# Two-layer hybrid mixer block on one core: halved filler units, two interleaved output units, bias rows read from PSUM, and four early units in the last norm

## The chip, the cores and the metric

The kernel runs on one core of a Trainium2 chip. The metric is the device time of one execution in microseconds, as the median of several runs. Lower is better.

## What is computed

Two layers of a transformer-like block over 256 latent tokens `x` and 256 context tokens `h`, model width 1024, hidden width 2816. Each layer has a half-step SwiGLU FFN, a token mixer and a second half-step SwiGLU FFN, each behind an RMS norm that is modulated per channel by vectors computed from `c` and `c_ctx`:

```python
x = x + 0.5 * mx[2] * swiglu(modulate(rms_norm(x, norm_ffn1[l]), mx[0], mx[1]), ffn1_w_in[l], ffn1_w_out[l])
ux = modulate(rms_norm(x, norm_mix[l]), mx[3], mx[4])
yx, yh = token_mixer(ux, uh, w_in[l], ...)
x = x + mx[5] * yx
x = x + 0.5 * mx[8] * swiglu(modulate(rms_norm(x, norm_ffn2[l]), mx[6], mx[7]), ffn2_w_in[l], ffn2_w_out[l])
```

The mixer projects its input once (`w_in`), runs three branches (a Fourier mix, grouped-query attention with 8 heads, neighbourhood attention with 4 heads), maps each to width 1024, merges them with three sigmoid gates computed from the same input, and multiplies by `w_o`. The context tokens go the same way in layer 0. In layer 1 they only supply keys and values, so most work there has 256 columns and not 512. A final RMS norm of `x` is the output.

## The kernel before

**Layout.** Activations are held with channels on partitions: `x`, `u_hi`, `u_lo` are 128 x 8 x 512 (latent tokens in columns 0 to 255, context in 256 to 511). Each weight block is one "unit" of 128 output channels: up to eight 128x128 blocks, 512 KB. Every product is made of three matmuls for the precision (`three_of`, L1286 to L1288): `w_hi*u_hi`, `w_hi*u_lo`, `w_lo*u_hi`. A unit of eight blocks is 24 matmuls.

**The weight ring.** Units pass in one fixed order through a ring of four slots. SyncE loads `w_raw`; ScalarE copies it to `w_hi` (`hi`, L526), which waits for the load and for TensorE to be done with the unit four places earlier (`w_used`); GpSimd subtracts to get `w_lo` (L494, two instructions of 128x512 for a unit, `w_lo_ready`); TensorE uses both. ScalarE's and VectorE's programs are written out in order, with the `hi` calls between the other work.

**Norms.** A norm is made without waiting for its root: while the layer's last product arrives in `x`, ScalarE and VectorE write `x * colA` as a pair (`first_scaled` L548, `first_split` L906), and TensorE runs the first two units of the next product (`pair` with `early`) on it, with two extra columns for the shift. `mean_square` (L1366), a root on ScalarE, and `spread` (L1373) give 1/rms on all partitions; then VectorE and ScalarE make the normalised operand `u_hi`, `u_lo` in eight steps (`norm`, L930, L581, L943). For an FFN the two early results are scaled at their eviction (`first_hidden`, L1017, L1023), and the product goes to `h_hi`, `h_lo` (L1005, L1007). TensorE's third step onward waits for `h_prod`; a shortcut for that step to wait only for the scaled halves applies where the step's number is a constant of the program. In the last norm (`k` = 5, the second FFN of layer 1, 256 tokens) the early pair lies in `u_hi`, `u_lo` itself.

**Attention.** The jobs go two at a time. Step `p` has, on TensorE: the transposes of the last step's first job, this step's scores, the transposes of the last step's second job, then units named by `between(l)` as fillers ("before"), the value matmuls of the last step (L1653), and more fillers ("after"). VectorE copies the transposed probabilities (L1199), takes maxima (L1155, L1156), and normalises (L1188); every second step in layer 0 and every step in layer 1 it also evicts a finished chunk to `cat_hi`, `cat_lo` (L1140, L1141). ScalarE copies the other half, takes the exponentials (L767), and evicts the fillers from bank 7 after them. In layer 0 even steps have the latent stream (512 keys) and odd ones the context stream (256 keys); steps 8 to 11 are the neighbourhood jobs, whose latent stream adds a bias first. The fillers are the remaining projections (`nk`, `nq`, `nv`, two each), the transposition of v (`vt`) and the first three gate units:

```python
return [([nk0], [nk1]), ([], []), ([nq0], []), ([], []), ([nq1], []), ([], []),
        ([nv0], [("vt", 1)]), ([nv1], [("vt", 2)]), ([g0], []), ([], []), ([g1], []), ([], []), ([g2], [])]
```

**Merge.** Eight gate steps follow; each ends with VectorE's merge (L1233, L1236, L1238, L1241, L1243) into one chunk of `mg_hi`, `mg_lo`. `w_o`'s first unit takes the chunks in order and so waits for the last; seven more units follow, alternating between banks 2 and 3, and each is added to `x` (`update`, L983), squared (L541), summed (L898) and split for the next norm (L906). ScalarE converts one unit of `w_o` in each of these steps.

**Start.** The per-channel rows (`vec`) are transposed into PSUM and copied to SBUF; `columns_norm(0)` (L876 to L878) combines them with the first modulation columns, and the first norm follows.

## Time and profile before

| | |
|---|---|
| median of 3 runs | 2025.54 us (2023.0 to 2025.99) |
| profiled execution, device time | 2022.01 us |
| its span, first to last instruction | 2020.2 us |
| mean granted TensorE clock | 0.996 |
| TensorE busy | 1962.2 us (97%) |
| weight loads busy | 1609.4 us (80%) |
| GpSimd busy | 1006.0 us (50%) |
| VectorE busy | 773.1 us (38%) |
| ScalarE busy | 655.2 us (32%) |

The profile is of one execution. Times inside it are microseconds from its first instruction. The busy time of an engine counts instructions in progress. Matmuls overlap each other, so their mean duration is longer than the step from one to the next. A granted clock of 1.00 is 2.4 GHz on TensorE and 0.50 is 1.2 GHz.

### The profile page before, as it was taken

To read this page: it belongs to the slowest core of one execution; us is meant where nothing else is said; L and a number is where in the kernel's file an instruction comes from. 1 tells how busy PE (TensorE), PEld (TensorE's weight loads), DVE (VectorE), ACT (ScalarE), POOL (GpSimd) and SP (SyncE) were. 2 spreads that over 40 slices of the span, in tenths; PEclk is the share of its full clock that TensorE was granted. 3 is DMA by queue.
4 is the path that set the end of the run, shared out by engine and by line. 5 is a ranking of instruction groups with operands and counts; after the bars stand their busy time and mean duration, and the time that the engine had idled before them with its cause. 6 is when DMAs were issued, how large, how long until landed. Compare 5 with 4: busy or idle time off the path is not lost.

```text
span 2020.2 us, 29286 instructions
## 1 busy us (share of the span) xinstructions
PE 1962.2 (97%) x10550; PEld 1609.4 (80%) x10550; DVE 773.1 (38%) x1278; ACT 655.2 (32%) x1031; POOL 1006.0 (50%) x835
## 2 busy tenths in 40 slices
PE   6999999999999999999999999999999899999998
PEld 4777777787667888877877887788778677998998
DVE  4322122357762224623122353221233875564214
ACT  3211211243452223412211243222123444444433
POOL 2444444343213544545544445454445433988997
PEclk9999999999999999999999999999999999999999
DMA  9555655343112333553354236434523422655664
GB/s 338 171 179 181 195 189 181 122 113 108 43 43 64 102 94 94 172 183 114 117 165 129 72 112 224 159 96 142 179 67 105 142 75 58 183 166 158 184 181 131
DMA packets 413575, 279.25 MB, mean 138 GB/s; under 512 B 25346, under 2 KB 398588, under 8 KB 406060
## 3 DMA queue, kind: packets, MB, share of 16 engines
q1 hardware_dynamic: 401868, 206.79, 34.6%
q10 hardware_dynamic: 11520, 71.05, 9.6%
q8 instruction: 62, 1.02, 0.2%
q14 instruction: 29, 0.24, 0.0%
q0 software_dynamic: 96, 0.16, 0.0%
HBM read 276.92 MB, written 1.05 MB: 138 GB/s over the span
## 4 chain that ended last, share of the span: by engine, by line
PE 84%; POOL 5%; issue 5%; DVE 4%; DMA 1%; ACT 1%; SPq 0%; POOLq 0%; DVEq 0%; ACTq 0%
PE bank L1286 26%; PE bank L1287 26%; PE bank L1288 25%; POOL w_lo L494 5%; PE bank L1395 3%; DVE u_lo L943 1%; PE bank L1653 1%; PE bank L1635 1%; PE bank L1588 1%; DMA w_raw<-in_ffn_w_in 1%; DVE tmp L930 1%; DVE rstd L1112 1%; PE bank L1535 1%; DVE qk L1103 0%; SPq L403 0%
## 5 line engine op out<-in xcount | busy, mean ns | idle before, releaser
L494 POOL TENSOR_TENSOR w_lo<-w_raw,w_hi 128x512 fp32r<-128x512 f32 (+2 forms) x824 | 1003.4, 1247 | 1003.0 <-ACT w_hi L526 1002.2
L1286 PE MATMUL bank<-u_hi,w_hi 128*128 128x512 f32 (+2 forms) x2008 | 723.2, 360 | 16.6 <-DVE u_lo L943 12.4
L1287 PE MATMUL bank<-u_lo,w_hi 128*128 128x512 f32 (+2 forms) x2008 | 713.7, 355 | 0.0
L1288 PE MATMUL bank<-u_hi,w_lo 128*128 128x512 f32 (+2 forms) x2008 | 712.9, 355 | 0.0
L1286 PEld LDWEIGHTS bank<-u_hi,w_hi 128*128 128x128 f32 x2008 | 380.6, 190 | 97.1 <-DVE hf L999 21.0
L526 ACT ACTIVATE w_hi<-w_raw 128x1024 fp32r<-128x1024 f32 (+2 forms) x412 | 385.3, 968 | 178.1 <-PE bank L1288 164.3
L1288 PEld LDWEIGHTS bank<-u_hi,w_lo 128*128 128x128 f32 x2008 | 380.5, 189 | 53.9
L1287 PEld LDWEIGHTS bank<-u_lo,w_hi 128*128 128x128 f32 x2008 | 380.9, 190 | 52.3 <-issue 0.8
L999 DVE TENSOR_TENSOR hf<-bank,sg 128x512 f32<-128x512 f32 (+1 forms) x85 | 53.2, 625 | 613.5 <-ACT sg L628 613.5
L1286 PE MATMUL bank<-h_hi,w_hi 128*128 128x512 f32 (+1 forms) x704 | 256.0, 364 | 0.0
L1287 PE MATMUL bank<-h_lo,w_hi 128*128 128x512 f32 (+1 forms) x704 | 255.4, 363 | 0.0
L1288 PE MATMUL bank<-h_hi,w_lo 128*128 128x512 f32 (+1 forms) x704 | 255.2, 363 | 0.0
L628 ACT ACTIVATE sg<-bank 128x512 f32<-128x512 f32 (+1 forms) x85 | 46.3, 544 | 638.3 <-PE bank L1288 638.3
L983 DVE SCALAR_TENSOR_TENSOR x<-bank,colG,x 128x256 f32<-128x256 f32 (+1 forms) x136 | 60.6, 480 | 276.3 <-PE bank L1288 275.7
L1286 PEld LDWEIGHTS bank<-h_hi,w_hi 128*128 128x128 f32 x704 | 132.9, 189 | 25.6 <-DVE x L983 5.0
L1288 PEld LDWEIGHTS bank<-h_hi,w_lo 128*128 128x128 f32 x704 | 132.9, 189 | 20.7
L1287 PEld LDWEIGHTS bank<-h_lo,w_hi 128*128 128x128 f32 x704 | 132.9, 189 | 20.4
L1007 DVE TENSOR_TENSOR h_lo<-hf,h_hi 128x512 fp32r<-128x512 f32 (+2 forms) x88 | 125.5, 1426 | 4.6
L541 ACT ACTIVATE sq<-x 128x512 f32<-128x512 f32 (+3 forms) x48 | 26.9, 560 | 179.4 <-DVE x L983 179.3
L1233 DVE TENSOR_TENSOR tmp<-bank,sig 128x512 f32<-128x512 f32 (+1 forms) x42 | 20.8, 551 | 161.5 <-PE bank L1288 161.5
L814 ACT ACTIVATE sig<-bank 128x512 f32<-128x512 f32 (+1 forms) x42 | 20.6, 491 | 160.0 <-PE bank L1288 160.0
L1395 PE MATMUL bank<-mod_w,sil 128*32 128x512 f32 x512 | 61.6, 598 | 0.0
(170 smaller groups left out, 1523.7 us busy)
## 6 DMA issues: line engine op xcount, KB each, us to landing
w_raw<-in_ffn_w_in SPq DMA_DIRECT2D x176, 512.0 KB, 3.8
mod_w<-in_mod_w ACTq DMA_DIRECT2D x56, 1024.0 KB, 6.9
w_raw<-in_w_in SPq DMA_DIRECT2D x68, 512.0 KB, 3.7
w_raw<-in_ffn_w_out SPq DMA_DIRECT2D x64, 384.0 KB, 3.4
w_raw<-in_ffn_w_out SPq DMA_DIRECT2D x64, 320.0 KB, 3.3
mod_first<-in_mod_w SPq DMA_DIRECT2D x4, 2048.0 KB, 14.3
mod_w<-in_mod_w ACTq DMA_DIRECT2D x16, 512.0 KB, 5.5
w_raw<-in_w_o SPq DMA_DIRECT2D x16, 512.0 KB, 4.2
```

What stands on the lines that cost most here:

```text
L494: pool.tensor_tensor(w_lo[:, slot, k0:k1, :], w_raw[:, slot, k0:k1, :], w_hi[:, slot, k0:k1, :].bitcast(F32), ALU.subtract).then_inc(S("w_ ...
L526: act.activation(w_hi[:, slot, 0:n, :], w_raw[:, slot, 0:n, :], ACT.Copy).then_inc(S("w_hi_ready"), 1)
L541: act.activation(sq[:, par, 0:n], x[:, bass.ds(m, 1), 0:n].rearrange("p a n -> p (a n)"), ACT.Square).then_inc(S("sq_ready"), 1)
L628: act.activation(sg[:, b, 0:n], bank[:, 2 * b + 1, 0:n], ACT.Silu).then_inc(S("silu_ready"), 1)
L983: last = dve.scalar_tensor_tensor(out=xs, in0=bank[:, b, cols], scalar=colG[:, k, v, bass.ds(m, 1)], in1=xs, op0=ALU.mult, op1=ALU.add)
L999: dve.tensor_tensor(hf[:, b, 0:n], bank[:, 2 * b, 0:n], sg[:, b, 0:n], ALU.mult).then_inc(S("h_prod"), 1)
L1007: dve.tensor_tensor(h_lo[:, bass.ds(s, 1), 0:n].rearrange("p a n -> p (a n)"), hf[:, b, 0:n], hs.bitcast(F32), ALU.subtract).then_inc(S("h ...
L1233: last = dve.tensor_tensor(tmp[:, j, 0:n], bank[:, 3 + j, 0:n], gates, ALU.mult)
L1286: pe.matmul(dst, w_hi[:, slot, kk, :], hi_, start=start, stop=False)
L1287: pe.matmul(dst, w_hi[:, slot, kk, :], lo_, start=False, stop=False)
L1288: return pe.matmul(dst, w_lo[:, slot, kk, :], hi_, start=False, stop=stop)
L1395: last = pe.matmul(bank[32 * q:32 * q + 32, 6, :].rearrange("p (a i) -> p a i", i=32), sil[:, 2 * b + par, :], w[:, q], start=b == 0 and p ...
```

## The change

- `between(l)` names three lists per step ("middle" comes between the two transpose groups), and most fillers are cut in two halves of four weight blocks (12 matmuls) each, which go to neighbouring steps. Bank 7 holds the sum between them, and the unit is evicted after its second half.
- `w_o`'s first two units run interleaved, block by block, on banks 2 and 6. ScalarE converts `w_o`'s third and fourth unit ahead of the first update of `x`, and stays one unit further ahead; the following phase's third unit is converted in the last step.
- `columns_norm(0)` reads the rows from PSUM (bank 4) and no longer from the copy in SBUF.
- In the last norm four units (two FFN steps) run on `x * colA`. It lies in its own tiles (`first_hi_m`, `first_lo_m`), and both steps are scaled at eviction, both scalings ahead of the first product.

```diff
         if l == DEPTH - 1:
-            return [([nk0], [nk1]), ([nq0], [nq1]), ([nv0], [("vt", 1)]), ([nv1], [("vt", 2)]), ([g0], []), ([g1], []), ([g2], [])]
-        return [([nk0], [nk1]), ([], []), ([nq0], []), ([], []), ([nq1], []), ([], []),
-                ([nv0], [("vt", 1)]), ([nv1], [("vt", 2)]), ([g0], []), ([], []), ([g1], []), ([], []), ([g2], [])]
+            return [([], [nk0], [nk1]), ([], [nq0], [nq1]), ([], [nv0], [vt1]), ([], [nv1], [vt2]),
+                    ([], [g0a], []), ([], [g0b], [g1a]), ([g1b], [g2a], [g2b])]
+        return [([], [nk0], [nk1]), ([], [nq0a], []), ([], [nq0b], []), ([], [nq1a], []), ([], [nq1b], []),
+                ([], [nv0a], []), ([], [nv0b], [vt1]), ([], [nv1a], []), ([], [nv1b], [vt2]),
+                ([], [g0a], []), ([], [g0b], []), ([], [g1a], []), ([g1b], [g2a], [g2b])]
...
+    def wo_bank(m):
+
+        return 6 if m == 1 else 2 + m % 2
...
     def first_x(k):
 
-        if norm_tokens(k) == SEQ:
-            return u_hi, u_lo
         return (first_hi_m, first_lo_m) if k % 3 == 2 else (first_hi_f, first_lo_f)
...
+    def first_steps(k):
+
+        return 2 if norm_tokens(k) == SEQ else 1
...
-                for q in (2, 3):
+                for q in (3,) if k % 3 == 2 else (2, 3):
                     hi(ph, q % ph.nu, q // ph.nu)
...
-                if k and n == SEQ and d == DC - 3:
-                    hi(ph, 4 % ph.nu, 4 // ph.nu)
+                if k and n == SEQ and d in (2, 5):
+                    q = 4 + d // 4
+                    hi(ph, q % ph.nu, q // ph.nu)
...
+            nph = phases[following(key)]
+            ahead = [(ph, q) for q in range(2, DC)] + [(nph, q) for q in range(3)]
+            hi(ph, 0, 1)
             for m in range(DC):
-                if m + 2 < DC:
-                    hi(ph, m % 2, (m + 2) // 2)
-                elif m + 2 == DC:
-                    first_hi(following(key))
+                p_, q = ahead[m + 1]
+                hi(p_, q % 2, q // 2)
                 square_at(out_step(l, 0) + m, DC * (k - 1) + m, m % 2, m, norm_tokens(k))
                 first_scaled(k, m)
...
+            rows = vec if k else vec_bank
+            gain = rows[:, l, V_N1 + DC * w + d0:V_N1 + DC * w + d1]
...
-                    if start and k:
-                        first_hidden()
-                    else:
-                        hidden(0 + i * 2, 0)
-                    hidden(1 + i * 2, 1)
+                    steps = first_steps(k) if start and k else 0
+                    for c in range(steps):
+                        first_scales(c)
+                    for c in range(2):
+                        if c < steps:
+                            first_hidden(c)
+                        else:
+                            hidden(c + i * 2, c)
...
-                    if k and half == 0 and isinstance(s, int) and s == 2:
+                    if k and half == 0 and isinstance(s, int) and 2 <= s < 2 + first_steps(k):
...
-            for p, (before, after) in enumerate(between(l)):
+            for p, (middle, before, after) in enumerate(between(l)):
                 if p == 1:
                     pe.wait_ge(S("qk_ready"), 5 * (l + 1))
                 if p:
                     transposes(2 * p - 2)
                 if p < NP:
                     scores(p)
+                for u in middle:
+                    fill(u)
...
+            slots, goals = zip(*(ph.at(j, 0)[:2] for j in range(2)))
+            pe.wait_ge(S("x_done"), m0)
+            for kk in range(DC):
+                if kk in (0, LO_SPLIT):
+                    pe.wait_ge(S("w_lo_ready"), goals[1] * 2 + (2 if kk else 1))
+                pe.wait_ge(S("mg_ready"), MG0 + kk + 1)
+                for j in range(2):
+                    last = three(bank[:, wo_bank(j), 0:n], slots[j], kk, mg_hi, mg_lo, kk, n, kk == 0, kk == DC - 1)
+                    if kk == DC - 1:
+                        last.then_inc(S("w_used"), 1)
+            for m in range(2, DC):
+                pe.wait_ge(S("x_done"), m0 + m - 1)
+                products(ph, m % 2, m // 2, 0, 2, bank[:, wo_bank(m), 0:n], mg_hi, mg_lo, 0, n, True, True)
```

## Rows read from the trace of the kernel before

**Rows 1.** The page: busy us of each engine.

```profile
PE 1962.2 (97%) x10550; PEld 1609.4 (80%) x10550; DVE 773.1 (38%) x1278; ACT 655.2 (32%) x1031; POOL 1006.0 (50%) x835
```

**Rows 2.** View of waits, TensorE: us in total, times, longest.

```profile
PE bank L1286 <- DVE u_lo L943: 12.4, 12, 5.5
...
PE bank L1653 <- DVE pT L1199: 4.5, 5, 0.9
...
PE bank L1635 <- DVE pT L1199: 3.7, 3, 2.0
PE bank L1286 <- DVE cat_lo L1141: 2.9, 2, 1.7
...
PE bank L1286 <- DVE mg_lo L1243: 2.2, 1, 2.2
...
PE bank L1286 <- DVE hf L1023: 1.8, 1, 1.8
```

**Rows 3.** Windows: length, busy us (instructions) by engine, granted clock, DMA.

```profile
660.00:680.00 20.00, 20.00 (x90) 16.57 (x89) 4.39 (x7) 5.27 (x7) 8.36 (x8) 1.00 0.36 105
...
1740.00:1760.00 20.00, 20.00 (x169) 20.00 (x169) 11.21 (x14) 8.35 (x12) 18.38 (x14) 1.00 0.67 196
...
1695.11:1698.44 3.33, 3.33 (x16) 3.33 (x17) 0.69 (x1) 0.60 (x1) 1.13 (x1) 0.50 0.17 50
...
31.41:36.15 4.74, 4.74 (x11) 3.78 (x12) 3.89 (x10) 2.76 (x5) 0.56 (x1) 0.50 1.05 404
...
513.37:612.26 98.89, 90.39 (x538) 63.33 (x537) 68.01 (x152) 50.38 (x130) 17.66 (x14) 1.00 0.13 38
```

**Rows 4.** Timeline of VectorE at the start: start, duration, instruction.

```profile
26.14 1.14 DVE L876 TENSOR_TENSOR colB<-modcol,vec 128x8 f32<-128x8 f32 x1
...
27.39 1.12 DVE L878 SCALAR_TENSOR_TENSOR colA<-colA,vec 128x8 f32<-128x8 f32 x1
...
44.65 0.17 DVE L876 TENSOR_TENSOR colB<-modcol,vec 128x8 f32<-128x8 f32 x1
```

**Rows 5.** Timeline of GpSimd at the start.

```profile
24.77 4.95 POOL L494 TENSOR_TENSOR w_lo<-w_raw,w_hi 128x512 fp32r<-128x512 f32 x4 [21.09 <-ACT w_hi L526]
```

**Rows 6.** Groups by line, VectorE, 1796.2 to 1816.5: busy us, mean ns.

```profile
L983 DVE SCALAR_TENSOR_TENSOR x<-bank,colG,x 128x256 f32<-128x256 f32 x6 | 2.8, 472 | 0.0
```

**Rows 7.** Timeline of VectorE, step 10 of layer 0's attention and after.

```profile
593.71 0.88 DVE L1188 TENSOR_SCALAR probs<-probs,rrec 128x512 f32<-128x512 f32 x2
...
595.32 0.88 DVE L1188 TENSOR_SCALAR probs<-probs,rrec 128x512 f32<-128x512 f32 x2
596.12 0.69 DVE L1140 CAST cat_hi<-bank 128x512 fp32r<-128x512 f32 x1
...
597.46 0.68 DVE L1199 COPY pT<-bank 128x512 f32<-128x512 f32 x1
```

**Rows 8.** Timeline of TensorE, the same stretch.

```profile
594.99 1.08 PE L1653 MATMUL bank<-pT,Vn 128*64 128x256 f32 x8
...
597.03 1.14 PE L1588 MATMUL bank<-nqk 64*128 64x256 f32 x8
```

**Rows 9.** Timeline of ScalarE, layer 1's attention, step 5.

```profile
1692.35 0.38 ACT L791 ACTIVATE sq<-bank 128x256 f32<-128x256 f32 x1
```

**Rows 10.** Timeline of VectorE, layer 1's last merge and first update.

```profile
1791.24 0.29 DVE L1241 CAST mg_hi<-tmp 128x256 f32 x1
1791.65 0.42 DVE L1243 TENSOR_TENSOR mg_lo<-tmp,mg_hi 128x256 f32 x1
...
1793.86 0.48 DVE L983 SCALAR_TENSOR_TENSOR x<-bank,colG,x 128x256 f32<-128x256 f32 x1
```

**Rows 11.** Timeline of GpSimd, the same stretch.

```profile
1796.22 4.17 POOL L494 TENSOR_TENSOR w_lo<-w_raw,w_hi 128x512 fp32r<-128x512 f32 x3 [5.42 <-ACT w_hi L526]
```

**Rows 12.** Timeline of VectorE, the last norm and its first hidden chunk.

```profile
1819.77 0.87 DVE L930 SCALAR_TENSOR_TENSOR tmp<-x,colA,bank 128x256 f32<-128x256 f32 x2 [1.78 <-PE bank L1373]
...
1833.07 1.26 DVE L1005 CAST h_hi<-hf 128x256 fp32r<-128x256 f32 x1
```

127 lines of the change are left out of this document (66 added, 61 removed).

## The prediction

> **What bounds the kernel now.** The page comes first: TensorE is busy for 1962.2 of 2020.2 us, GpSimd for half of that, and the other two engines for less [rows 1]. So the change, which adds no matmul and removes none, can only take from the 58 us in which TensorE does nothing, or add to them. The view of waits, for TensorE alone, says who ends those gaps [rows 2]: VectorE in nearly all of them. The u_lo row is the norms: 5.5 us of its 12.4 is the start, most of the rest the norm of layer 1's mixer, which stays as it is. The rows on L1653 and L1635 are attention steps without a filler, cat_lo is the end of attention, mg_lo the last merge, and hf the last norm. The windows give the stages' sizes [rows 3]: in 98.9 us of layer 0's attention TensorE is busy for 90.4, which leaves 8.5 us. In the same rows 90 matmuls of 512 columns take 20 us (0.222 us each), 169 of 256 columns 20 us (0.118 us). They also show the clock: after a gap of 2.0 us the granted clock was 0.50 (the lower level, 1.2 GHz) for 3.33 us, in which 16 matmuls ran; at 1.00 they take 1.9 us, so this fall cost 1.4 us. After the 5.5 us gap at the start it stayed at 0.50 for 4.74 us, with 11 matmuls of 512 columns (0.43 each); 3.4 us of that instead of 0.222 cost 1.6 us.
>
> **Bias rows in PSUM.** Two of the three small operations on columns at the start take 1.14 and 1.12 us, and the first of them takes 0.17 at 44.65 us, with GpSimd idle [rows 4]; at the start GpSimd subtracts from 24.77 to 29.72 us [rows 5]. With one operand in PSUM they read SBUF once. Such an operation is not slowed beside a busy GpSimd: the update of x at L983 has one operand in PSUM, and took 0.47 us on the mean of six while GpSimd ran [rows 6]. That frees 0.97 + 0.95 = 1.9 us. But the chain goes on to u_lo, which reads two tensors of SBUF, and would come 1.9 us earlier, some 1.2 us before 29.72: it waits for the fourth subtraction, and about 1 us goes back. I take -0.9 us for TensorE's first start. Bounds: 0, if all goes back, and -1.9.
>
> The Trainium skill (SBUF — State Buffer, Who interferes with whom) says that a VectorE instruction with two SBUF inputs and a GpSimd instruction that reads SBUF exclude each other for a whole instruction. The trace agrees, 1.14 against 0.17 us; by the rule alone the term would be the full -1.9 only if u_lo, too, met no subtraction. The same rule speaks against the earlier conversion below.
>
> **Half fillers, layer 0.** No work is added, so only the stalls count. Before, they are 4.5 us in five empty steps (0.9 each, before the value matmuls), 1.7 of the 3.7 us before transposes, 1.7 of the 2.9 us before cat, and 0.6 in pieces under 0.25 us, together 8.5 [rows 2, 3]. A half filler (12 x 0.222 = 2.7 us) covers each 0.9, and at the end g2's second half covers the 1.7. But half the filler is also taken from every even step, which has 512 keys and the heavy softmax. Step 10 shows it [rows 7, 8]. Its value matmuls start at 594.99 behind a full filler; with half, at 592.3, and end at 593.3. The next transposes need probabilities that VectorE has normalised only at 593.71 + 0.88 = 594.6: 1.3 us late. Eight transposes (from the end of the value matmuls to 597.03, 1.0 us) and scores (1.14) bring TensorE to 596.8. The second transposes need the copy of the first, and that stands on VectorE behind the second normalise (to 596.2), the two cat operations (1.34) and itself (0.68), so 598.2: 1.5 us late. Before, these two steps had 0.1 + 0.9; now 2.9: +1.9.
>
> The others, by the same steps: without a bias to add (1.4 us less on VectorE in this chain) the first stall is gone. Steps 4/5: 1.5 against 1.0, +0.5; steps 2/3, with a mask operation in the chain, 2.2 against 2.0, +0.2. In steps 6 and 8 a transposition of v follows the second half, and it needs bank 7 evicted. ScalarE evicts behind both exponentials. In step 10 these end by 595.1, since VectorE's second normalise starts at 595.32 [rows 7]; an eviction of 256 columns takes 0.38 us [rows 9], one of 512 by that some 0.6, so it ends at 595.7. Half a filler earlier TensorE arrives at 593.3 and waits 2.4 us; no stall follows. Step 8 is such a step: 2.4 against 1.0 before for its pair, +1.4. In step 6, without bias, 1.0 against 0. Step 1: -0.9. Step 12: 0.2 against 2.3, -2.1. Sum: 1.9 + 0.5 + 0.2 + 1.4 + 1.0 - 0.9 - 2.1 = +2.0, and six more starts of an accumulation at under 0.1 us, +0.5: **+2.5 us**. Bounds: -8.5, all stalls of rows 3 gone, and +5.5, if the clock falls behind both stalls over 2 us (1.6 each). I stay by the VectorE chain, whose rows I have in order.
>
> **Half fillers, layer 1.** Step 4 loses half of g0, but a VectorE chain bounded it within 0.2 us, so nothing moves. In step 5 g1's first half waits until g0 is evicted, behind the exponentials, at 1692.73 [rows 9]; TensorE, which before had done step 5 by 1692.0 (1695.11 less the gap of 2.0 and eight transposes of 1.1 [rows 2, 3]), is half a gate lighter (1.4) and about 0.4 late for a copy: it stands from 1691.0. Then half a gate (1.4), eight transposes, half a gate, transposes (1.0 each), half a gate, values 1.9, half a gate: the gate stage starts at 1692.8 + 9.7 = 1702.5; before, it was 1703.6, with a clock fall of 1.4 us inside. If this stall of 1.8 us makes the clock fall, 1.1 us of gain turn into +0.3. Even odds: **-0.5 us**, bounds -1.1 and +0.4 (-3 us, the waits before transposes and cat, is the end from below).
>
> **Merge and last norm.** Interleaving two units gives 42 matmuls of cover (5.0 us from 1787.2) in place of 21, and the 2.2 us wait for mg_lo, which ended at 1792.07, would go [rows 2, 10]. But ScalarE now converts wo's fourth unit as soon as gate's last unit is used (1787.2) and not at 1795.1. GpSimd, which then stood for 5.42 us [rows 11], subtracts from 1790.8 to 1793.7. In that stretch VectorE has the cast and the subtraction of the last merge, 0.29 and 0.42 us with GpSimd idle [rows 10]; a cast of the same size beside a busy GpSimd took 1.26 [rows 12], and the subtraction behind it waits for the second half. So mg_lo comes near 1794.0, the update of x at 1795.8 in place of 1793.86 [rows 10], and the third unit waits for that update. VectorE and GpSimd then go in step, 2.88 us for a unit as TensorE does, so the lateness of 1.9 us shrinks little up to the mean square: by the start of the norm's VectorE part I keep 0.7 late (1820.4 for 1819.77 [rows 12]), since TensorE starts its units on x some 0.9 us earlier (GpSimd resumes 1.9 us later but one unit of 2.88 us further on, and that was what TensorE waited for).
>
> The norm itself is VectorE's, 13.3 us from there to the end of step 0's product just before the cast at 1833.07 [rows 12], and TensorE's third step waits for that product (the 1.8 us on hf [rows 2]; its step number is a register, so the shortcut for the first steps doesn't apply). Four units on x remove the waits for u_lo before it, but the third step starts no earlier: two more scalings (0.8) come ahead of the product, and two conversions go into the norm. Together with fewer subtractions around the product itself the third step starts 0.7 us later, and TensorE stands: from 1814.1 the first pair takes 6.9 us with the mean square and the spread, the second 5.7 (48 x 0.118), to 1826.7, and the third step starts at 1833.9, some 7 us later. After 5.5 us of standing the clock took 4.74 us to rise [rows 3]; behind 7 us I expect a fall again, at 256 columns 1.4 to 2.1 us, 1.8 taken. Together **+2.5 us**. Bounds: -4 (mg_lo's 2.2 and hf's 1.8 gone, clock kept) and +4.5. In layer 0's wo a unit has 5.3 us, both gain and delay are hidden.
>
> **Sum.** -0.9 + 2.5 - 0.5 + 2.5 = +3.6 us. The profiled execution took 2022.0 us, 1.8 around its span, and lies 3.5 under the median of the runs. On the median this is 2025.5 + 3.6 = 2029.1 us, 0.18% slower, just inside 0.2% (4.05 us), which is about what a measurement here tells from none.
>
> **The rivals.** (1) The stalls cost more: the clock also falls behind layer 0's stalls of 2.2 and 2.4 us in steps 3 and 8, 1.6 each: 3.6 + 3.2, 2032.3. One of them is enough to be over 4.05. For it: a gap of 2.0 did it [rows 3]. Against: behind the 2.2 us on mg_lo the clock stayed. (2) The fillers do what they are for: the five waits before the value matmuls go and no other takes their place, -4.5; with -0.9 at the start, -0.5 in layer 1, and the last part at nothing, 2025.5 - 5.9 = 2019.6. It decides if step 10's transposes wait under 0.5 us. For it: the 0.9 us covers are certain. Against: the order in rows 7. (3) The fillers cost what I say, but the merge is not delayed, the third step starts 1.5 earlier, and the clock holds: -0.9 + 2.5 - 0.5 - 1.5 = -0.4, 2025.1. (4) The conversion comes no earlier, because its weights land late: like (3), but the clock's 1.8 is paid: 2026.9.
>
> **Chances.** Forecast (0 to +4.05) 0.36; rival 1 and all of over +4.05, 0.36; rivals 3 and 4 0.14; rival 2 0.14. Within 0.2%: 0.36 + 0.12 = 0.48, with a little of rivals 3 and 4 falling out faster; slower 0.36; faster 0.16. The range, 2020 to 2034, reaches to rival 2 from below and over rival 1; the forecast's own is 2025.5 to 2030.
>
> **What the new profile would show.** Right: VectorE's first column operations under 0.3 us; TensorE waits of 1 to 2.5 us before transposes in odd steps and before the turning of v; the cast of mg_hi over 1 us with GpSimd's subtraction beside it; TensorE idle for 5 us or more before the third step of the last FFN, with the clock at 0.50 behind. Wrong: no stalls in steps 6 to 11 of layer 0, or the third step starting over 2 us earlier relative to the last merge.

## The result: 0.18% slower

The changed kernel took 2026.85 us (median of 20 runs, 2022.93 to 2029.23) against 2023.4 us for the kernel before on the same chips (20 runs, 2020.08 to 2026.47). The ratio, which compares each run with runs of the kernel before on its own chip, is 1.0018, 95% interval 1.0012 to 1.0024. That is +3.6 us on 2023.4; the plain difference of the two medians is 3.45. The prediction counted from an earlier median of three runs, 2025.54, so its 2029.1 lies 2.2 us over the measured 2026.85 while its difference fits. The profiled execution took 2028.1 us, its span is 2026.1 us, and the mean granted clock 0.993. That is 5.9 us more span than before; the medians differ by less, since the profiled execution of before lay 1.4 us under its median here and that of the changed kernel 1.3 over its own.

The page, busy us of each engine; it answers to [rows 1]:

```profile
PE 1966.7 (97%) x10550; PEld 1612.6 (80%) x10550; DVE 775.4 (38%) x1280; ACT 654.8 (32%) x1031; POOL 1006.8 (50%) x835
```

The view of waits, TensorE; it answers to [rows 2]:

```profile
PE bank L1320 <- DVE u_lo L968: 9.0, 8, 4.7
...
PE bank L1667 <- DVE pT L1232: 5.0, 3, 2.2
...
PE bank L1320 <- DVE hf L1053: 4.5, 1, 4.5
...
PE bank L1639 <- ACT tmp L739: 3.2, 2, 2.3
...
PE bank L1667 <- DVE probs L1221: 2.3, 2, 1.3
PE bank L1320 <- ACT sq L811: 2.1, 2, 1.8
PE bank L1320 <- DVE x L1009: 1.6, 2, 1.3
PE bank L1320 <- DVE mg_lo L1276: 1.5, 1, 1.5
```

The 4.5 us in which the value matmuls waited for pT in five steps are gone, and so are the two waits for cat_lo. In their place stand 5.0 us before transposes that wait for the copied probabilities (pT), 2.3 before transposes that wait for the normalised ones (probs; 1.3 of them in layer 0), 3.2 before the turning of v (tmp), and 1.8 us behind one eviction in layer 1 (sq). In the last stage hf, the first hidden chunk, is up from 1.8 to 4.5, and mg_lo is down from 2.2 to 1.5, with 1.3 of the 1.6 us for x beside it. Two waits there have shrunk: that for u_lo (12.4 to 9.0 in all; 2.5 of the 12.4 were in the last norm, and none is now) and that for w_lo (2.1 to 0.2); one of 1.3 us for the sum of squares is new.

Windows of the changed kernel: layer 0's attention from the first scores to the first gate step, the two times the clock was at its lower level in it, layer 1's attention from and to the same, the last stage (from w_o's first product in layer 1 to the last FFN's first output product), and the start and the last norm at the lower level:

```profile
496.15:617.38 121.23, 111.01 (x617) 76.56 (x617) 82.23 (x174) 55.46 (x141) 21.32 (x17) 0.97 0.14 40
531.59:535.00 3.41, 3.41 (x10) 2.64 (x10) 2.92 (x9) 2.53 (x9) 0.00 (x0) 0.50 0.54 154
579.38:582.79 3.41, 3.41 (x18) 2.91 (x18) 2.19 (x4) 1.72 (x3) 2.50 (x2) 0.50 0.00 0
1629.64:1707.74 78.10, 74.11 (x474) 55.58 (x473) 54.42 (x102) 38.58 (x81) 23.82 (x18) 1.00 0.19 55
1791.26:1891.08 99.82, 91.08 (x728) 90.03 (x727) 52.47 (x92) 44.86 (x67) 80.56 (x61) 0.97 0.53 152
30.52:36.66 6.14, 6.14 (x16) 4.01 (x20) 3.88 (x10) 2.77 (x5) 1.96 (x2) 0.50 1.04 400
1836.70:1842.31 5.61, 5.61 (x26) 5.61 (x27) 3.64 (x5) 1.55 (x2) 4.92 (x4) 0.50 0.28 83
```

The same three stages before:

```profile
496.04:612.26 116.22, 107.58 (x618) 75.56 (x617) 82.86 (x174) 59.07 (x145) 21.27 (x17) 1.00 0.14 42
1624.31:1703.64 79.33, 75.66 (x473) 56.61 (x473) 54.34 (x102) 41.29 (x87) 23.76 (x18) 0.98 0.21 61
1787.23:1885.12 97.89, 89.29 (x729) 87.76 (x728) 52.92 (x90) 44.65 (x67) 80.29 (x61) 1.00 0.53 156
```

So layer 0's attention is 5.0 us longer, layer 1's 1.2 shorter, and the last stage 1.9 longer. In the last stage TensorE idles as long as before (99.82 less 91.08 is 8.7 us, 97.89 less 89.29 is 8.6): the 1.9 us there are the clock's. From TensorE's last modulation matmul at the start to the first FFN's output product both kernels take 143.2 us (25.87 to 169.08, and 25.88 to 169.09), and layer 0's merge has a new wait of 0.36 us for the update of x. 0 + 5.0 + 0.3 - 1.2 + 1.9 = 6.0 us.

### The profile page after: what moved, and what is told of

The parts are those of the page before. It is cut to its first block, busy times and chain, and to the rows that moved or that the text cites. A ratio compares the mean times of both kernels' runs of the same rounds, so it can differ in the third digit from the quotient of the medians.

```text
span 2026.1 us, 29233 instructions
## 1 busy us (share of the span) xinstructions
PE 1966.7 (97%) x10550; PEld 1612.6 (80%) x10550; DVE 775.4 (38%) x1280; ACT 654.8 (32%) x1031; POOL 1006.8 (50%) x835
## 4 chain that ended last, share of the span: by engine, by line
PE 89%; DVE 6%; issue 1%; ACT 1%; SPq 1%; DMA 1%; DVEq 0%; ACTq 0%
PE bank L1320 28%; PE bank L1321 27%; PE bank L1322 27%; PE bank L1425 3%; PE bank L1618 1%; PE bank L1667 1%; PE bank L1685 1%; DVE smax L1189 1%; DVE u_lo L968 1%; DMA mod_first<-in_mod_w 1%; SPq L415 1%; DVE tmp L955 1%; DVE rstd L1145 1%; PE bank L1565 1%; DVE qk L1136 0%
## 5 line engine op out<-in xcount | busy, mean ns | idle before, releaser
L1320 PE MATMUL bank<-u_hi,w_hi 128*128 128x512 f32 (+1 forms) x1976 | 715.7, 362 | 16.0 <-DVE u_lo L968 9.0
L1321 PE MATMUL bank<-u_lo,w_hi 128*128 128x512 f32 (+1 forms) x1976 | 706.9, 358 | 0.0
L1322 PE MATMUL bank<-u_hi,w_lo 128*128 128x512 f32 (+1 forms) x1976 | 706.1, 357 | 0.0
L1320 PEld LDWEIGHTS bank<-u_hi,w_hi 128*128 128x128 f32 x1976 | 376.1, 190 | 96.6 <-DVE hf L1025 21.0
L1322 PEld LDWEIGHTS bank<-u_hi,w_lo 128*128 128x128 f32 x1976 | 376.2, 190 | 54.1
L1321 PEld LDWEIGHTS bank<-u_lo,w_hi 128*128 128x128 f32 x1976 | 376.4, 190 | 51.9 <-issue 0.5
```

The costliest lines, as they stand in the source:

```text
L1320: pe.matmul(dst, w_hi[:, slot, kk, :], hi_, start=start, stop=False)
L1321: pe.matmul(dst, w_hi[:, slot, kk, :], lo_, start=False, stop=False)
L1322: return pe.matmul(dst, w_lo[:, slot, kk, :], hi_, start=False, stop=stop)
```

## The new profile in the four places

**Start.** VectorE's timeline; it answers to [rows 4]:

```profile
26.13 0.16 DVE L901 TENSOR_TENSOR colB<-modcol,bank 128x8 f32<-128x8 f32 x1
...
26.40 0.16 DVE L903 SCALAR_TENSOR_TENSOR colA<-colA,bank 128x8 f32<-128x8 f32 x1
```

GpSimd's, which answers to [rows 5]:

```profile
24.75 4.94 POOL L510 TENSOR_TENSOR w_lo<-w_raw,w_hi 128x512 fp32r<-128x512 f32 x4 [21.08 <-ACT w_hi L542]
```

Both operations on the bias rows take 0.16 us with GpSimd subtracting. TensorE's first product starts at 30.52 us in place of 31.41. But the clock stayed at 0.50 for 6.14 us behind it (4.74 before, [rows 3]), and at 40.40 TensorE waited:

```profile
40.40 0.64 PE L1412 MATMUL bank<-mod_first,sil 128*32 128x512 f32 x4 [0.20 <-DMA mod_first<-in_mod_w]
```

**Layer 0, steps 8 and 10.** TensorE's timeline; it answers to [rows 8]:

```profile
579.10 0.84 PE L1639 MATMUL bank<-ident,tmp 128*128 128x128 f32 x4 [2.35 <-ACT tmp L739]
...
597.10 1.09 PE L1667 MATMUL bank<-ident,probs 128*128 128x128 f32 x8 [1.27 <-DVE probs L1221]
...
600.73 1.06 PE L1667 MATMUL bank<-ident,probs 128*128 128x128 f32 x8 [1.47 <-DVE pT L1232]
```

VectorE's in step 10, which answers to [rows 7]:

```profile
596.16 0.88 DVE L1221 TENSOR_SCALAR probs<-probs,rrec 128x512 f32<-128x512 f32 x2
...
597.78 0.88 DVE L1221 TENSOR_SCALAR probs<-probs,rrec 128x512 f32<-128x512 f32 x2
...
599.90 0.68 DVE L1232 COPY pT<-bank 128x512 f32<-128x512 f32 x1
```

The three stalls are 2.35, 1.27 and 1.47 us, where 2.4, 1.3 and 1.5 were foreseen. The transposes at 597.10 start when VectorE's first normalise of the step has ended (596.16 and 0.88 us), and those at 600.73 when the copy at 599.90 has, which stands behind the second normalise and the two cat operations, as in the prediction's order. The other stalls were 2.23 us in step 3 (2.2 foreseen), 1.35 in steps 4 and 5 (1.5) and 0.88 in step 6 (1.0).

**Last merge.** VectorE's timeline, which answers to [rows 10], and GpSimd's, which answers to [rows 11]:

```profile
1795.29 1.16 DVE L1274 CAST mg_hi<-tmp 128x256 f32 x1
1796.58 1.28 DVE L1276 TENSOR_TENSOR mg_lo<-tmp,mg_hi 128x256 f32 x1
...
1799.63 0.48 DVE L1009 SCALAR_TENSOR_TENSOR x<-bank,colG,x 128x256 f32<-128x256 f32 x1
```

```profile
1785.56 12.01 POOL L510 TENSOR_TENSOR w_lo<-w_raw,w_hi 128x512 fp32r<-128x512 f32 x9
```

GpSimd subtracts until 1797.57, 6.3 us after w_o's first product. In the kernel before it had stopped 3.6 us after it (at 1790.80, [rows 11]), ahead of the cast at 1791.24. The cast takes 1.16 us in place of 0.29 and the subtraction behind it 1.28 in place of 0.42. Counted from w_o's first product, mg_lo is ready after 6.6 us (4.8 before) and the first update starts after 8.4 (6.6 before).

**Last norm.** VectorE's part starts and its product stands at these rows, which answer to [rows 12]; then TensorE's third step:

```profile
1824.23 0.87 DVE L955 SCALAR_TENSOR_TENSOR tmp<-x,colA,bank 128x256 f32<-128x256 f32 x2 [1.37 <-PE bank L1403]
...
1836.07 0.48 DVE L1053 SCALAR_TENSOR_TENSOR hf<-hf,shift_sum,sg 128x256 f32<-128x256 f32 x1
```

```profile
1836.70 0.58 PE L1320 MATMUL bank<-u_hi,w_hi 128*128 128x256 f32 x1 [4.52 <-DVE hf L1053]
```

TensorE stands 4.52 us, and then the clock is at 0.50 for 5.61 us.

## The experiments

All ratios are to the kernel before on the same chip, with 95% intervals; each kernel has one profiled execution. The first seven kernels differ from the changed kernel in one edit each, the last five combine edits.

### Layer 0's fillers whole again

```diff
-        return [([], [nk0], [nk1]), ([], [nq0a], []), ([], [nq0b], []), ([], [nq1a], []), ([], [nq1b], []),
-                ([], [nv0a], []), ([], [nv0b], [vt1]), ([], [nv1a], []), ([], [nv1b], [vt2]),
-                ([], [g0a], []), ([], [g0b], []), ([], [g1a], []), ([g1b], [g2a], [g2b])]
+        return [([], [nk0], [nk1]), ([], [], []), ([], [nq0], []), ([], [], []), ([], [nq1], []),
+                ([], [], []), ([], [nv0], [vt1]), ([], [nv1], [vt2]), ([], [g0], []),
+                ([], [], []), ([], [g1], []), ([], [], []), ([], [g2a], [g2b])]
```

> The changed kernel with layer 0's fillers back in whole units at their old steps; only g2 stays in two halves around the last value matmuls. Mine: the halves take cover from the even steps. First scores to gate stage took 121.2 us with the halves (116.2 before); it comes to 114.5 here: the waits before transposes and before the turning of v (2.2, 1.35, 0.9, 2.35, 1.3, 1.5 us) go, five waits of 0.9 come back, the 1.7 us at the end stays covered, and the clock stays at 1.00 in this stage. About 6.5 us less than the changed kernel's profile, 4 to 5 on the median, so 0.05 to 0.1% under the kernel before. Rival (the halves cost only because the clock fell twice by chance): 118 us, and no change but the two falls. Rival (something else of the change costs): 121.

Measured 2021.7 us, ratio 0.9991 (0.9982 to 1.0000), 5.5 us under the changed kernel's ratio. Its attention stage, and a stretch within it:

```profile
496.29:612.45 116.16, 109.27 (x617) 76.57 (x617) 82.94 (x174) 56.40 (x141) 21.25 (x17) 0.99 0.14 42
532.94:536.35 3.41, 3.41 (x17) 2.15 (x14) 2.33 (x8) 1.23 (x6) 0.00 (x0) 0.50 0.37 110
```

The 0.9 us waits are back, and the stage is 5.1 us shorter than with halves. It is as long as before, not 1.7 us shorter as expected with g2 still halved: the clock fell here once, behind waits of 1.12 and 0.89 us. In the two executions with the same fillers whose clock held (the best version and the same with early conversions, below) it took 114.5 us, so that g2's halves alone are worth 1.7 us, as foreseen for the end. The rival that the halves cost only through two falls of the clock wanted 118 us and is refuted: this stage took 116.2 with a fall in it.

### The turning of v one step later

```diff
-                ([], [nv0a], []), ([], [nv0b], [vt1]), ([], [nv1a], []), ([], [nv1b], [vt2]),
-                ([], [g0a], []), ...
+                ([], [nv0a], []), ([], [nv0b], []), ([vt1], [nv1a], []), ([], [nv1b], []),
+                ([vt2], [g0a], []), ...
```

> The changed kernel with the two turnings of v one step later, ahead of the second transposes of steps 7 and 9, when their unit is long evicted. Mine: VectorE's chain is as long as ScalarE's, so the waits of 0.9 and 2.35 us before the turning go but waits before the transposes of steps 7 and 9 come (1.4 and 1.3 + 1.5 us): first scores to gate stage within 1 us of 121.2, less up to 1.6 us if the clock does not fall. Rival (ScalarE's queue, an eviction behind the exponentials, is what costs in steps 6 and 8): 3.2 us less, 118, and no new waits.

Measured 2026.38 us, ratio 1.0017 (1.0007 to 1.0026). The stage, and TensorE's timeline in steps 8 and 9:

```profile
495.39:613.43 118.04, 108.15 (x617) 74.06 (x617) 82.32 (x174) 55.34 (x141) 21.32 (x17) 1.00 0.14 41
```

```profile
575.68 1.09 PE L1667 MATMUL bank<-ident,probs 128*128 128x128 f32 x8 [1.27 <-DVE probs L1221]
...
579.30 0.95 PE L1667 MATMUL bank<-ident,probs 128*128 128x128 f32 x7 [0.89 <-DVE pT L1232]
```

The wait of 2.35 us on the eviction is gone, and 1.27 + 0.89 us before the transposes around it have come in its place. TensorE idles 9.9 us in the stage, after 10.2. So the eviction was only who came last: the pair of steps is as long as VectorE's chain. This stage also shows what the halves cost with the clock at 1.00 throughout: 118.0 us, 1.8 more than before. In that sum g2's halves gain 1.7 us; against the 114.5 us of whole fillers with g2 halved, the other halves cost 3.5.

### w_o's conversions one place later

```diff
             for m in range(DC):
-                p_, q = ahead[m + 1]
-                hi(p_, q % 2, q // 2)
+                if m:
+                    p_, q = ahead[m]
+                    hi(p_, q % 2, q // 2)
                 square_at(out_step(l, 0) + m, DC * (k - 1) + m, m % 2, m, norm_tokens(k))
                 first_scaled(k, m)
+            p_, q = ahead[DC]
+            hi(p_, q % 2, q // 2)
```

> The changed kernel with ScalarE's conversions in the output product one place later, so that GpSimd has nothing to do beside the last merge, as before the change. Mine: the cast of mg_hi takes 0.29 and not 1.16 us, mg_lo 0.42 and not 1.28; mg_lo ends 4.9 us after the output product's start (6.6 in the changed kernel), the first update of x begins 6.6 us after it (8.4), the 1.45 us wait at the eighth block is gone. The norm's units then wait for GpSimd again, so the third step of the last FFN comes only 0.4 to 1 us earlier (45.4 us after the output product's start in the changed kernel). Rival (the slow cast is not GpSimd's doing): the same durations, and no gain.

Measured 2026.41 us, ratio 1.0018 (1.0009 to 1.0028). VectorE's timeline at the last merge, then TensorE's at the norm's first unit:

```profile
1793.76 0.29 DVE L1277 CAST mg_hi<-tmp 128x256 f32 x1
1794.18 0.43 DVE L1279 TENSOR_TENSOR mg_lo<-tmp,mg_hi 128x256 f32 x1
...
1796.38 0.48 DVE L1012 SCALAR_TENSOR_TENSOR x<-bank,colG,x 128x256 f32<-128x256 f32 x1
```

```profile
1817.49 0.36 PE L1323 MATMUL bank<-first_hi_m,w_hi 128*128 128x258 f32 x1 [2.69 <-POOL w_lo L510]
```

GpSimd stood from 1793.34 to 1798.74 in this execution. With it standing, the cast takes 0.29 us again and the subtraction 0.43, and nothing else was changed there; beside GpSimd they took 1.16 and 1.28. The Trainium skill (SBUF — State Buffer, Who interferes with whom) gives the rule, an exclusive lock on the port pair that the two engines share, and these rows agree. mg_lo is 1.7 us earlier, but GpSimd's work is only done later, and at the norm's first unit TensorE waits 2.69 us for it. The third step of the last FFN starts 45.2 us after w_o's first product, against 45.4 in the changed kernel, which is less than the 0.4 to 1 us expected: the early conversion costs 1.7 us where it stands and 0.25 us at the end, and the time is that of the changed kernel.

### Two units on x in the last norm

```diff
     def first_steps(k):
-        return 2 if norm_tokens(k) == SEQ else 1
+        return 1
```

> The changed kernel with two units on x in the last norm in place of four (its own tiles kept). Mine: the norm is VectorE's chain, so the third step starts no later, and 0.4 to 0.8 us earlier, because one scaling less stands ahead of the product; TensorE works through the norm with pieces of waiting under 1.5 us, the clock stays at 1.00 behind it (5.6 us at 0.50 in the changed kernel), worth 2.4 us. About 3 us less in all. Rival (the four units give what they are for): the third step starts 2 us later or more, and the gain of the clock is used up by that.

Measured 2024.23 us, ratio 1.0004 (0.9995 to 1.0013), 2.8 us under the changed kernel. The last stage:

```profile
1793.70:1890.81 97.11, 89.72 (x729) 87.83 (x727) 51.69 (x90) 44.71 (x67) 80.34 (x61) 1.00 0.53 157
```

97.1 us, 2.7 less than in the changed kernel and 0.8 less than before, with five waits under 1 us in place of one of 4.5 (those for mg_lo, x and the sum of squares stay), and the clock at 1.00. The third step starts 45.2 us after w_o's first product, 0.26 earlier than with four units (0.4 to 0.8 expected) and not 2 us later, as the rival had it. The four units on x are thus the costly part of the last stage, and the interleaved merge is not: it gives the 97.1 us with the clock held.

### Bias rows from SBUF again

```diff
-            rows = vec if k else vec_bank
+            rows = vec
```

> The changed kernel with the bias rows read from the copy in SBUF again, as before. Mine: the earlier start of 0.9 us (first product at 30.52 for 31.41 us) goes away, and yet the work that follows is not later, because the time was given back before 40.5 us: the clock stayed at 0.50 for 6.1 us behind the start (4.7 before) and TensorE waited 0.2 us for the first modulation part. So the output product of the first FFN half starts at 169.1 within 0.2 us as in both kernels, and the run's time is within 0.05% of the changed kernel's. Rival, the prediction's own term: the edit is worth 0.9 us, the mark comes at 170.0 and the time rises by 0.04 to 0.05%; the time alone can't tell them, the mark does.

Measured 2027.4 us, ratio 1.0016 (1.0007 to 1.0025). TensorE's first gap is 5.54 us again, as before the change (4.65 in the changed kernel). From the last modulation matmul to the first output product this execution took 142.75 us (25.53 to 168.28), the changed kernel 143.21 and the kernel before 143.22. The mark was 168.3 and not within 0.2 of 169.1, so the numbers of the first theory were missed, but not towards the rival, which wanted 0.9 us more. Three things add up in this stretch, and each was read in several executions. The gap is 0.9 us shorter with PSUM rows in all 12 executions that have them. The time that the clock stays at 0.50 behind the first product differs between executions of the same code: 6.1 us in the changed kernel, 3.5 in the best version below, whose start is the same code (30.14 to 33.65), 3.6 here. And TensorE waits for the first modulation part between 35 and 43 us in 10 of the 12 executions with the earlier start, by 0.2 to 2.5 us, 0.86 on the mean of the 12, and in neither of the two with the later one. So the 0.9 us are won, and then waited away: the whole stretch took 142.1 to 146.7 us in the 12 executions with the rows in PSUM, median 143.0, and 142.75 and 143.22 in the two with the rows in SBUF.

### The third step freed of the product

```diff
-                bodies(pe, FH // 2, body, mods, peel=half == 0)
+                bodies(pe, FH // 2, body, mods, peel=(2 if k == 5 else 1) if half == 0 else 0)
```

(the same on ScalarE and VectorE; the number of the third step becomes a constant, so that the shortcut applies)

> The changed kernel with the second body of the last FFN's first half written out too, so that the third step's number is a constant and it waits only for the two scaled halves and no longer for the product. Mine: the third step starts when the second up scaling has ended, 1.05 us ahead of the first product's end in the changed kernel (1835.49 against 1836.54), so 1.0 us earlier, TensorE stands 3.5 us in place of 4.5, and the end comes 1.0 us earlier (0.05%), or up to 3 us if 3.5 us no longer make the clock fall. Rival: the fourth step's bank or the split behind the product is late next and takes the 1.0 us back, so nothing is gained.

Measured 2025.28 us, ratio 1.0005 (0.9996 to 1.0014), 2.6 us under the changed kernel. TensorE's timeline and the window behind it:

```profile
1836.06 0.55 PE L1319 MATMUL bank<-u_hi,w_hi 128*128 128x256 f32 x1 [3.43 <-DVE sg L1042]
```

```profile
1836.06:1839.47 3.41, 3.41 (x16) 3.41 (x17) 3.31 (x7) 2.51 (x4) 1.62 (x2) 0.50 0.52 153
1791.75:1889.47 97.72, 90.10 (x729) 89.08 (x727) 52.44 (x92) 44.75 (x67) 80.25 (x61) 0.98 0.53 156
```

The step starts with the second up scaling, 44.3 us after w_o's first product (45.4), and stands 3.4 us in place of 4.5. The clock is low for 3.4 us behind it and not for 5.6. The last stage is 2.1 us shorter: 1.1 from the wait and 1.0 from the clock. The rival, a late bank or split that takes the gain back, didn't come.

### Layer 1's fillers whole again

```diff
-                    ([], [g0a], []), ([], [g0b], [g1a]), ([g1b], [g2a], [g2b])]
+                    ([], [g0], []), ([], [g1], []), ([], [g2], [])]
```

> The changed kernel with layer 1's fillers whole at their old steps; layer 0's halves and all else stay. Mine: the 1.8 us wait behind the eviction of g0 goes, the waits before the transposes and before cat return (2.0 and 1.7 us), so from the first scores to the gates 79.3 us in place of 78.1 if the clock falls there again, 78.0 if it doesn't: the time is up by 0 to 1.2 us (0 to 0.06%). Rival, that the halves in layer 1 cost as they do in layer 0: the stage gets shorter by 1 us or more.

Measured 2027.48 us, ratio 1.0017 (1.0008 to 1.0026).

```profile
1629.20:1707.03 77.83, 74.14 (x474) 55.06 (x473) 54.33 (x102) 41.34 (x87) 23.80 (x18) 1.00 0.21 62
```

77.8 us with the clock at 1.00, where the halves take 78.1 us and the kernel before took 79.3 with a fall. The wait of 2.0 us before the transposes was there in this execution and in the one before, and the clock fell behind it in only one of them. So layer 1's halves don't shorten the stage, they cost 0.3; what they took away in the profile was a fall of the clock, and that one doesn't come in each execution. The rival, a stage shorter by 1 us or more without them, is refuted; the time alone (1.0017 against 1.0018) shows no difference.

### What gained, put together

Four edits in one kernel ("the best version"): layer 0's fillers whole again, w_o's conversions one place later, two units on x, and the third step freed of the product.

> What gained and what cost nothing, together: layer 0's fillers whole at their old steps but for the last, whose halves stay, layer 1's halves kept, the interleaved merge kept with ScalarE's conversions one place later, two units on x in the last norm, and the third step freed of the product. By the runs so far: changed kernel 1.0018 of before, less 0.0027 for layer 0's fillers, less 0.0014 for two units, less 0.0005 for the third step: 0.9972 of before, some 2018 us, with 116 us from the first scores to the gates in layer 0. Rival, that the savings are the same time counted twice (each only fills a wait that the others leave): 0.9985 or more.

Measured 2019.01 us, ratio 0.9976 (0.9966 to 0.9986).

```profile
494.92:609.44 114.52, 107.63 (x618) 75.62 (x617) 82.83 (x174) 56.40 (x141) 21.24 (x17) 1.00 0.15 42
...
1783.52:1880.56 97.04, 90.70 (x729) 89.20 (x728) 49.84 (x90) 44.47 (x67) 80.01 (x61) 0.98 0.54 157
```

Layer 0's attention is 1.7 us under before and the last stage 0.9 under; layer 1's took 78.1 us (1621.88 to 1700.00). The savings of the two layers add. Those inside the last stage do not, in this profile: two units on x gave 97.1 us alone, and with the freed third step and the late conversions it is 97.0, with one fall of the clock in it. So the rival, the same time counted twice, is partly right there, and the interval just reaches its 0.9985. The same with the early conversions of the changed kernel:

> The best version so far with ScalarE's conversions at the changed kernel's early places again (the only difference). There the late places removed the 1.4 us wait at the eighth block but gave 2.7 us of waiting for GpSimd at the norm's first unit. Mine: the conversions' order only moves one wait along this chain, since GpSimd and VectorE have the same work in either order: from w_o's first product to the last FFN's output product within 0.6 us of the best version's 97.0, the ratio within 0.0005 of its 0.9976. Rival, that the early conversion is what the merge pays with: 1.5 us or more longer.

Measured 2017.44 us, ratio 0.9974 (0.9963 to 0.9984); the last stage took 96.2 us (1784.21 to 1880.41). That is 0.8 under the late order, more than the 0.6 allowed, and the times can't tell the two apart. The rival, 1.5 us longer, is refuted. It is also 0.9 under the 97.1 us of two units alone, which has the same order of conversions. The freed third step is the difference between the two in this stage, so in this order it adds something, even with the clock at 0.50 twice. And with w_o's first two units one after the other:

```diff
-            for kk in range(DC):
-                ...
-                for j in range(2):
+            for j in range(2):
+                for kk in range(DC):
```

> The best version with w_o's first two units one after the other again, as before the change; banks and all else stay. Mine: the interleaving is worth the 2.2 us wait for the last chunk of the merge, less what returns as a wait for the update of x (1.25 us in the best version): from w_o's first product to the last FFN's output product 0.5 to 1.5 us longer than 97.0, a ratio 0.0003 to 0.0007 above 0.9976. Rival, that the wait only moves to GpSimd and VectorE behind it: no difference.

Measured 2019.12 us, ratio 0.9982 (0.9973 to 0.9991); the last stage took 1.4 us more than in the best version, and the wait of 2.2 us for mg_lo is back:

```profile
1786.18:1884.64 98.46, 91.98 (x728) 90.65 (x727) 48.85 (x90) 44.48 (x67) 79.07 (x61) 0.97 0.53 155
```

But TensorE idles 6.5 us in it (98.46 less 91.98), against 6.3 in the best version. The 2.2 us for mg_lo stand in place of 1.25 us for x, and the next wait, for w_lo, is 2.0 in place of 2.7. What is longer is the time with the clock at 0.50: 6.8 us, with one fall behind the 2.2 us, against 3.4. So in waits interleaving gains only 0.1 us, as the rival had it (the wait moves on); the 0.5 to 1.5 us expected came, but by way of the clock. What it takes away is a wait of 2.2 us behind which the clock fell here and stayed in the kernel before. In the times the two intervals overlap.

### Fillers cut at a quarter

The best version, with six matmuls of each filler in the odd step and eighteen in the even one:

```diff
+        def pieces(u):
+            return [(u[0], u[1], 0, 0.5), (u[0], u[1], 0.5, 2)]
...
+            (nq0a, nq0b), (nq1a, nq1b), (nv0a, nv0b), (nv1a, nv1b) = (pieces(u) for u in (nq0, nq1, nv0, nv1))
+            (g0a, g0b), (g1a, g1b) = (pieces(u) for u in (g0, g1))
...
-                part = (LO_SPLIT * begun, LO_SPLIT * done)
+                part = (int(LO_SPLIT * begun), int(LO_SPLIT * done))
```

> The best version with layer 0's fillers cut at two of eight blocks instead of whole: six matmuls (1.33 us) go to the odd step, where 0.89 us are waited before the value matmuls, and eighteen stay in the even step. Mine (a filler half is too large a piece: it covers 0.9 us with 2.7 and takes 2.7 from the step with the heavy softmax): the 0.89 us waits go, the stalls before transposes and before the turning of v stay under those of the changed kernel by 1.0 to 1.3 each, so that the stage from the first scores to the gates takes 113 to 115 us against the best version's 114.5 and the changed kernel's 121.2 (118.0 where its clock held). Rival, that any cut filler costs as much as a halved one, because a chain through VectorE sets the pairs of steps whatever TensorE does: 118 us or more.

Measured 2015.84 us, ratio 0.9963 (0.9950 to 0.9977). The stage, and TensorE's timeline, the rows with a wait:

```profile
495.99:607.95 111.96, 107.58 (x617) 74.11 (x617) 82.50 (x174) 56.01 (x141) 21.31 (x17) 1.00 0.15 43
```

```profile
529.31 1.07 PE L1675 MATMUL bank<-ident,probs 128*128 128x128 f32 x8 [1.12 <-DVE pT L1240]
...
572.65 0.63 PE L1647 MATMUL bank<-ident,tmp 128*128 128x128 f32 x4 [1.00 <-ACT tmp L744]
...
591.29 1.06 PE L1675 MATMUL bank<-ident,probs 128*128 128x128 f32 x8 [1.46 <-DVE pT L1240]
```

111.96 us, under the 113 to 115 expected: all waits of 0.9 us before the value matmuls are gone, and of the stalls in the stage only three over 0.4 us are left: 1.12, which the kernel before had too, 1.00 and 1.46. TensorE idles 4.4 us in the stage, against 8.6 before and 10.2 with halves. Of the 4.3 us under before, 1.7 are g2's halves; the finer cut itself gives 2.6 (112.0 for 114.5). The three edits that gained, on the changed kernel:

> The changed kernel with three edits: layer 0's fillers cut at two of eight blocks, two units on x in the last norm, and the third step freed of the product; the conversions stay early, as in the change. Mine: both parts add, 112.0 us from the first scores to the gates in layer 0 and 96.2 us from w_o's first product to the last FFN's output product, against 121.2 and 99.8 in the changed kernel: about 0.996 of before, some 10 to 11 us under the changed kernel. Rival, that the gain of the finer cut came from that execution's clock alone: 0.9975 or more.

Measured 2015.19 us, ratio 0.9960 (0.9946 to 0.9973): 111.97 us in layer 0's attention (495.87 to 607.84) and 96.3 us in the last stage (1781.71 to 1878.01), both as expected, and 0.0058 under the changed kernel, 11.7 us. This version beats both kernels.

## Why the prediction was right, point by point

The sign and the size came out as forecast (+3.6 us and +3.6 us by the ratio), and the mechanism, VectorE's chain in layer 0 and a stand with a fall of the clock in the last norm, is what the trace shows. But the terms did not come out one by one, and in the last stage two misses cancel. That the sum meets the forecast to a tenth is luck: the profile's terms sum to 6.0 us, and the measured interval is 2.4 to 4.9.

| term | predicted | profile | what the other runs add |
|---|---|---|---|
| start | -0.9 | 0.0 | the gap is 0.9 shorter in 12 of 12 executions, given back on the mean |
| layer 0's attention | +2.5 | +5.0 | +1.8 with the clock held; 120.0 us on the mean of the seven executions with halves, +3.8 |
| layer 0's merge | 0 | +0.3 | 0.36 us wait for x |
| layer 1's attention | -0.5 | -1.2 | +0.3 with the clock held |
| last merge and norm | +2.5 | +1.9 | 99.3 to 100.7 us in five executions with this code, mean 99.9: +2.0 |

**Start.** The mechanism held: 0.16 us beside a busy GpSimd, and about 1 us given back at u_lo, whose two operations from 28.44 took 1.93 us beside GpSimd's fourth subtraction and 0.87 at 31.08, after it. What failed is the tacit step from "TensorE starts earlier" to "the end comes earlier". TensorE waited some 10 us later for a transfer, 0.86 us on the mean of the 12 executions. The prediction had put this wait at nothing, without a reason.

**Layer 0.** The order of the VectorE chain held for each stall, within 0.15 us where it was given. TensorE's idle time in the stage rose by 1.6 us (10.2 against 8.6), where the pairs sum to 2.0. No run shows the +0.5 for six more starts of an accumulation: TensorE was busy for 108.15 us in the one execution with halves whose clock held (v turned later), 0.6 over before, but the quarter cuts have as many starts and the same 107.58 us as before. The remaining 2.9 us (111.01 less 108.15) are rival 1: the clock fell behind the stalls of steps 3 and 8, the two places that it named. Over the seven executions with halves it fell behind step 3's in five, and behind step 8's in four of the six that have it; with whole fillers, behind the 1.12 and 0.89 us of step 3 in two of five. So the forecast and rival 1 both describe executions with these fillers, and a chance for "the clock falls" should have been a share of the runs and not one case or the other. Rival 2 is refuted for halves: the transposes of its test waited 1.27 us, and it needed less than 0.5. With the piece cut smaller most of it happens: the waits before the value matmuls go and smaller ones take their place, 2.6 us gained beside g2's 1.7. One slip in the sum: the upper bound, 2.5 and two falls at 1.6, is 5.7 and not 5.5.

**Layer 1.** The gate stage came 9.64 us after the eviction's wait ended (9.7 foreseen), and the stall of 1.78 us that was to have even odds on a fall brought one in one of 12 executions. (The pieces listed for the 9.7 us add up to 9.5.) But whole fillers with the clock held take 77.8 us, so the gain in the profile is the fall that the kernel before had, and the halves themselves gain nothing.

**Merge and norm.** The cast, the subtraction and the update came as worked out, late by 1.7 to 1.8 us (1.9 foreseen). What failed is "the third step starts 0.7 us later": it starts 0.5 us earlier than before relative to w_o (45.4 for 46.0). VectorE's part of the norm did start later, by 0.4 us (33.0 us after w_o's first product for 32.5; 0.7 foreseen), but it was shorter. The norm's VectorE part took 12.3 us from its start to the end of step 0's product, where 13.3 and 0.8 for two more scalings were foreseen. The scalings added 0.7 us. Against that the product took 1.0 us less, the wait of 0.31 us for ScalarE before it is gone, and the eight steps took 0.2 less. GpSimd stood around the product:

```profile
1831.54 2.80 POOL L510 TENSOR_TENSOR w_lo<-w_raw,w_hi 128x512 fp32r<-128x512 f32 x2 [0.81 <-ACT w_hi L542]
1837.39 5.43 POOL L510 TENSOR_TENSOR w_lo<-w_raw,w_hi 128x512 fp32r<-128x512 f32 x4 [3.05 <-ACT w_hi L542]
```

The product took 0.48 us with nothing beside it. In the kernel before it took 1.48, from 1831.55, with GpSimd subtracting from 1827.39 to 1838.22 without a pause. TensorE's stand was 4.5 us and not 7: the step came 1.2 us sooner than foreseen (45.4 for 46.7 us after w_o's first product), and the four units before it ended 1.4 us later (40.9 for 39.5), since TensorE waited 1.27 us inside them for the sum of squares, a wait that the prediction put at nothing. The clock's term was 1.8 and measured some 2.5 (26 matmuls in 5.61 us, at 0.12 each 3.1). So a later step and a shorter fall were foreseen, an earlier step and a longer fall came, and the sum is off by only 0.6. Of the signs that were to show the forecast right, "idle for 5 us or more before the third step" was missed with 4.5; the others came, and neither sign of being wrong did.

Rival 3 needed the clock to hold and the merge to be in time, and neither came. Rival 4 asked for weights that land late; the conversion was early.

**The sum.** The profile's +6.0 us and the runs' +3.6 differ because one profile of each kernel holds or lacks whole falls of the clock; 2.9 of the 6.0 are two such falls. Means over the executions at hand give 0 + 3.1 + 0.3 - 0.4 + 2.0 = 5.0 us, just over the upper end of the measured 2.4 to 4.9 (0.0012 and 0.0024 of 2023.4). Here 3.1 is 120.0 less 116.2 and less 0.6, two fifths of a fall of 1.6 for the two in five with whole fillers, and -0.4 is 78.2 (78.1 and one fall in 12) less the mean of 79.3 and 77.8. For the last stage of the kernel before there is only one execution, without a fall, and falls came in that stage in 12 of the 13 others; so the 2.0 may be too large. How much is not shown.

## What to carry to other kernels

Size a filler by the wait it is to cover. Against waits of 0.9 us, pieces of 1.3 us of matmuls took 2.6 us out of the stage (114.5 to 112.0), while pieces of 2.7 us took the cover from the next step and cost 3.5 (114.5 to 118.0), and the clock on top. A stall of about 2 us costs its length, and in 9 of 13 cases here some 1.5 us more through the clock, so one profile of each kernel overstates or hides such an edit by a few us; compare the stages of several executions. More work ahead of a wait gains nothing where the chain behind the wait gets the extra work too: four early units made one stand of 4.5 us out of waits that two units spread, with the same idle time as the kernel before and a fall of the clock behind it.

## What the runs showed of the hardware

- The same gap lowers the clock in some executions and not in others. The gap of 2.23 us in step 3 did in five of seven; that of 2.2 us for mg_lo did not in the kernel before and did in the best version without interleaving; the one of 1.78 us in layer 1 did in one of 12. When it fell behind these, it stayed at 0.50 for 3.41 us. Behind the stand of 3.8 to 4.6 us before the third step it stayed low for 6.8 us in all six executions that have it (1835.48 to 1842.31 in the changed kernel), and for 3.41 where the stand was 3.43.
- Behind the same gap of 4.65 us at the start the clock rose at any time between 33.6 and 36.7 us. The Trainium skill (TensorE: Matmul & The Clock Gate, Part 1: The HAM clock gate) says that this point varies from run to run of one kernel; these runs agree.
- A cast of 128x256 from SBUF to SBUF took 0.29 us alone and 1.16 to 1.26 beside GpSimd's subtractions, though it has a single input. The Trainium skill (SBUF — State Buffer, Who interferes with whom) lists casts among the operations that can take the shared pair, and these rows agree.
